# A retention and sliding-window attention trunk: the first retention head of each block goes from seven products with weight sums to eight plain ones

## What is computed

```
layer 0, retention (4 heads, q and k 256 wide, v and gate g 512 wide each):
  h = x @ ret_w_in ;  q, k, v, g = split(h) ;  q, k = rope(q), rope(k) / 16
  per chunk: inner = (q k^T * decay) v ; cross = (q state) * xi
             state = state * g_chunk + (k * zeta)^T v
  r = normalise(inner + cross) ;  x = post_norm(x, (silu(g) * r) @ ret_w_out)
shared keys and values:  kv = x @ swa_w_kv   (4 kv heads, 64 wide)
layer 1, sliding-window attention (16 heads, window of 2 chunks of 64, sinks, relative bias):
  x = post_norm(x, (attention(x) * silu(gate)) @ swa_w_out)
```

## Time and profile before

| | us |
|---|---|
| median of 3 runs | 2418.47 |
| profiled execution | 2420.02 |
| its span, first to last instruction | 2418.1 |
| PE busy | 2322.8 (96%) |
| DVE busy | 1799.0 (74%) |
| ACT busy | 1195.3 (49%) |
| POOL busy | 340.8 (14%) |

### The profile page before, as it was taken

The page is one execution under the profiler, slowest core; times in us unless marked ns, Lnnn a source line. Parts: engine busy times, 40 slices in busy tenths (PEclk is TensorE's granted clock), DMA queues, the critical chain, the costliest instruction groups (busy, mean ns, idle before and its releaser), DMA issues.

```text
span 2418.1 us, 31064 instructions
## 1 busy us (share of the span) xinstructions
PE 2322.8 (96%) x11506; PEld 1889.1 (78%) x11506; DVE 1799.0 (74%) x2589; ACT 1195.3 (49%) x1777; POOL 340.8 (14%) x350
## 2 busy tenths in 40 slices
PE   7888989999999999999999999999999999999996
PEld 5677778877778888887777888888777888888775
DVE  7877878875886668884687666887478667788458
ACT  3433445347644445535754544553665445554463
POOL 4122111203001110111201011110120110011031
PEclk9999999999999999999999999999999999999998
DMA  9886676772664445754284544585248345354423
GB/s 331 280 299 251 228 243 219 251 261 70 235 209 148 131 131 174 255 159 153 92 287 144 170 146 133 169 278 179 75 152 274 116 138 166 124 191 147 122 79 122
DMA packets 215062, 443.38 MB, mean 183 GB/s; under 512 B 15041, under 2 KB 52433, under 8 KB 211329
## 3 DMA queue, kind: packets, MB, share of 16 engines
q1 hardware_dynamic: 200832, 375.58, 47.3%
q0 software_dynamic: 14080, 65.83, 7.4%
HBM read 379.75 MB, written 57.41 MB: 181 GB/s over the span
## 4 chain that ended last, share of the span: by engine, by line
PE 70%; DVE 15%; DMA 6%; issue 4%; ACT 3%; SPq 1%; POOL 0%; DVEq 0%; ACTq 0%; POOLq 0%
PE accs L663 19%; PE accs L664 19%; PE accs L665 19%; DVE w_lo L1301 4%; DMA stage<-t_prep 3%; PE bank L663 2%; PE bank L665 2%; PE bank L664 2%; ACT w_hi L972 2%; PE bank L890 2%; PE bank L899 1%; PE bank L909 1%; PE bank L754 1%; DMA stage<-ret_w_in 1%; PE bank L842 1%
## 5 line engine op out<-in xcount | busy, mean ns | idle before, releaser
L1301 DVE TENSOR_TENSOR w_lo<-stage,w_hi 128x1024 fp32r<-128x1024 f32 x536 | 668.4, 1254 | 367.8 <-ACT w_hi L972 366.7
L972 ACT ACTIVATE w_hi<-stage 128x1024 fp32r<-128x1024 f32 x536 | 561.9, 1058 | 468.4 <-DMA stage<-t_prep 224.4
L663 PE MATMUL accs<-w_hi,xs 128*128 128x512 f32 x1120 | 447.9, 400 | 30.8 <-ACT sg L977 9.5
L665 PE MATMUL accs<-w_hi,xs 128*128 128x512 f32 x1120 | 441.2, 394 | 0.0
L664 PE MATMUL accs<-w_lo,xs 128*128 128x512 f32 x1120 | 440.3, 393 | 0.0
L663 PEld LDWEIGHTS accs<-w_hi,xs 128*128 128x128 f32 x1120 | 213.1, 190 | 81.0 <-issue 28.7
L665 PEld LDWEIGHTS accs<-w_hi,xs 128*128 128x128 f32 x1120 | 212.7, 190 | 45.9
L663 PE MATMUL accs<-x_hi,w_hi 128*128 128x512 f32 (+1 forms) x640 | 245.6, 384 | 1.2 <-ACT sgT L977 0.8
L664 PEld LDWEIGHTS accs<-w_lo,xs 128*128 128x128 f32 x1120 | 213.3, 190 | 42.5
L1961 POOL TENSOR_TENSOR rstd<-ve,half 128x1 f32<-128x1 f32 x96 | 79.4, 828 | 1176.0 <-DVE ve L1357 951.4
L664 PE MATMUL accs<-x_lo,w_hi 128*128 128x512 f32 (+1 forms) x640 | 237.5, 371 | 0.0
(11 more groups left out here) (193 smaller groups left out, 3866.9 us busy)
## 6 DMA issues: line engine op xcount, KB each, us to landing
stage<-t_prep SPq DMA_DIRECT2D x224, 512.0 KB, 4.4
stage<-ret_w_in SPq DMA_DIRECT2D x96, 512.0 KB, 3.9
stage<-ret_w_in SPq DMA_DIRECT2D x128, 256.0 KB, 3.0
stage<-swa_w_in SPq DMA_DIRECT2D x64, 512.0 KB, 4.1
t_prep<-t_buf POOLq DMA_DIRECT2D x28, 1024.0 KB, 6.1
stage<-ret_w_out SPq DMA_DIRECT2D x48, 512.0 KB, 3.7
cs<-rope_t SPq DMA_DIRECT2D x16, 1024.0 KB, 7.5
t_buf<-ret_w_in POOLq DMA_DIRECT2D x32, 512.0 KB, 9.8
```

Of the source, the lines that this page charges most:

```text
L663: mm(dst, lhs[0], rhs[0], start=start, stop=False, skip_group_check=reopened)
L665: return mm(dst, lhs[1], rhs[0], start=False, stop=stop, skip_group_check=reopened)
L972: copy(w_hi[:, g % HS], stage[:, g % LS], ACT.Copy).then_inc(w_hi_made, 1)
L1301: nc.vector.tensor_tensor(w_lo[:, g % LS], stage[:, g % LS], w_hi[:, g % HS].bitcast(F32), sub).then_inc(w_split, 1)
```

## The change

The first head of every block (`plain_head`) computes v and g by eight plain slots of 24 matmuls (4 banks x 2 k tiles x 3) from raw weights and raw x, 192 in place of 168. Slots `VG+8` to `VG+13` of head 0 are vacant: no engine has weight work there, and the ring is counted over the 128 slots that are left (`RING`, `ahead`, `before`), so that head 1's first pairs follow directly.

With it:
- v goes from the banks straight to `v_hi` and `v_lo`, the gate by one Silu from the banks to `sg`; the four sums over partial products and the extra copies of that head are gone. `score(H, 0)` stands at `VG+2`, `retain` at `VG+4`, `VG+5`, `VG+6`.
- Sets 0 to 3 are not made at all. The other 24 are made at other slots; for some the first two of the four operations and the last two stand at different slots ("begin" and "end").
- Block 0's x sums are made by DVE before the first slot, and their splits stand one to two slots earlier. In later blocks two of the four loads of x sums stand at slots 6 and 9 in place of 1 and 3.
- The unused `w_cache` path is removed.

```diff
+PLAIN = range(VG, VG + 8)
+VACANT = range(VG + 8, HEAD)
+PLAIN_BLOCKS = 4
+def vacant(g):
+    return g // NP < PLAIN_BLOCKS and g % NP in VACANT
+REAL = [g for g in range(NS * NP) if not vacant(g)]
+RING = {g: n for n, g in enumerate(REAL)}
+def ahead(g, n=AHEAD):
+    return REAL[RING[g] + n] if g in RING and RING[g] + n < len(REAL) else NS * NP
...
-T_PLAN = [(0, 0, -1, 1), (1, 1, -1, 1), (2, 2, -1, 2), (3, 3, -1, 2), (4, 0, 8, 11), (5, 1, 9, 13), (6, 2, 10, 14),
+T_PLAN = [(4, 0, 0, -1, 4, 4), (5, 1, 0, -1, 5, 5), (6, 2, 0, 1, 6, 6), (7, 3, 0, 2, 7, 7), (8, 0, 0, 6, 9, 10),
+          (9, 1, 0, 7, 11, 11), (10, 2, 0, 8, 18, 18), (11, 3, 0, 9, 19, 19), (12, 0, 0, 12, 19, 19), (13, 1, 0, 13, 20, 20),
+          (14, 2, 0, 20, 29, 31), (15, 1, 0, 22, 31, 34), (16, 3, 0, 21, 36, 36), (17, 2, 0, 33, 37, 37),
+          (18, 3, 0, 38, 47, 49), (19, 2, 0, 39, 49, 52), (20, 3, 0, 51, 54, 54), (21, 2, 0, 54, 56, 56),
+          (22, 3, 0, 56, 65, 65), (23, 3, 0, 67, 72, 72),
...
+def retain_slots(H):
+    return (VG + 4, VG + 5, VG + 6) if plain_head(H) else (VG + 7, VG + 10, VG + 13)
...
+            def plain_vg_pair(s, p):
+                j, i = divmod(p - VG, 4)
+                wait_weights(s * NP + p)
+                for m in range(4):
+                    if i == 0:
+                        fill = VG + (4 * j if m < 2 else 2 + 4 * j)
+                        need(pe, acc_free[m], prior(s, fill, m))
+                    for u in range(2):
+                        k = 2 * i + u
+                        phys = m // 2 if k < 4 else (2, 6)[m // 2]
+                        cols = slice(m % 2 * P, (m % 2 + 1) * P)
+                        mm = mm3(acc[m], (xs[:, phys, 0, k % 4, cols], xs[:, phys, 1, k % 4, cols]), weights(s * NP + p, u),
+                                 k == 0, k == KD - 1)
+                    if m == 1:
+                        mm.then_inc(products, 1)
+                mm.then_inc(products, 1 if p < PLAIN[-1] else 1 + 2 * len(VACANT))
...
+                        if v == 4 and plain_head(H):
...
+                            act.wait_ge(products, used(s * NP + VG + 2) + 1)
+                            copy(v_hi[:, 0:2, :], accs[:, 0:2, :], ACT.Copy).then_inc(v_hi_made, 1)
+                            act.wait_ge(products, used(s * NP + VG + 3))
+                            copy(v_hi[:, 2:4, :], accs[:, 2:4, :], ACT.Copy).then_inc(v_hi_made, 1)
+                            make_hi(ahead(g))
...
+                        if plain_head(H) and v == 4:
+                            nc.vector.tensor_tensor(v_lo[:, 0:2, :], accs[:, 0:2, :], v_hi[:, 0:2, :].bitcast(F32),
+                                                    sub).then_inc(x_free, 2)
+                            dve.wait_ge(v_hi_made, 2 * H + 2)
+                            nc.vector.tensor_tensor(v_lo[:, 2:4, :], accs[:, 2:4, :], v_hi[:, 2:4, :].bitcast(F32),
+                                                    sub).then_inc(y_free, 2)
```

More of the change, by code:

```diff
@@ L122, with before, plain, plain_head @@
 AHEAD, LOAD_AHEAD = 3, 4
[L124 to L135, removed]
+PLAIN = range(VG, VG + 8)
[7 more added lines that the diff above has]
+    return REAL[RING[g] + n] if g in RING and RING[g] + n < len(REAL) else NS * NP
+def before(g, n):
+    return REAL[RING[g] - n] if RING[g] >= n else -1
+def plain(s, p):
+    return s < PLAIN_BLOCKS and p in PLAIN
+def plain_head(H):
+    return H % RH == 0 and H // RH < PLAIN_BLOCKS
+def in_seven(H):
+    return H + 1 - min(H // RH + 1, PLAIN_BLOCKS)
 def loads(g):
-    return 2 if ready_made(g) or PAIRS[g % NP][0] == "qk" else 1
-LOADED, KEEPS, SPLITS = [], [], []
+    return 0 if vacant(g) else 2 if PAIRS[g % NP][0] == "qk" else 1
+LOADED, SPLITS = [], []
 for _g in range(NS * NP):
-    LOADED.append((LOADED[_g - LS] if _g >= LS else 0) + 16 * loads(_g))
-    KEEPS.append((KEEPS[_g - LS] if _g >= LS else 0) + 32 * to_keep(_g))
-    SPLITS.append((SPLITS[-1] if SPLITS else 0) + (not ready_made(_g)))
+    LOADED.append(0 if vacant(_g) else (LOADED[before(_g, LS)] if RING[_g] >= LS else 0) + 16 * loads(_g))
+    SPLITS.append((SPLITS[-1] if SPLITS else 0) + (not vacant(_g)))
 def n_state(n):
@@ L386, in last_set, with weight_pair @@
         def last_set(b):
[L388 to L393, removed]
+            return [n for n, buf, _, load, _, _ in T_PLAN if buf == b and load < RO][-1]
         def set_of(kind, h):
             return {"vg": 4 * h, "ro": RO_SET, "so": SO_SET}[kind]
-        def weight_pair(p, part):
+        def weight_pair(s, p, part):
+            if plain(s, p):
+                j, i = divmod(p - VG, 4)
+                return w_vg[:, i // 2, 2 * (i % 2):2 * (i % 2) + 2, j, 0, :]
             kind, c, q, i = PAIRS[p]
@@ L926, in _ @@
                         continue
-                    if kind in ("vg", "ro", "so"):
+                    if plain(s, p):
+                        plain_vg_pair(s, p)
+                    elif vacant(s * NP + p):
+                        continue
+                    elif kind in ("vg", "ro", "so"):
                         strassen_pair(s, p)
@@ L1756, in _ @@
                             if h == 0:
-                                make_lo(g + AHEAD)
-                        if v == 3:
+                                make_lo(ahead(g))
+                        if not plain_head(H) and v == 3:
                             dve.wait_ge(products, full(s, p, 1))
@@ L1778, in _ @@
                                 .then_inc(y_free, 2)
-                        if v == 11:
+                        if not plain_head(H) and v == 11:
                             after_retain(H, 1)
@@ L1994, in _ @@
                 pool.wait_ge(x_loaded[w], 16)
-            for n in range(4):
-                load_t(n)
+            for n, _, in_block, at_slot, _, _ in T_PLAN:
+                if at_slot < 0:
+                    load_t(n, in_block, at_slot)
             pool.wait_ge(init_done, 3)
```

296 lines of the change are left out of this document (151 added, 145 removed), and 5 rows, old and new, of the table T_PLAN.

## The result

| | before | changed |
|---|---|---|
| median of 19 runs each, us | 2420.28 | 2427.27 |
| lowest and highest, us | 2417.20, 2429.98 | 2423.69, 2430.38 |
| profiled execution: time, span, us | 2420.02, 2418.1 | 2430.38, 2428.3 |

The ratio is 1.0023, 95% interval [1.0016, 1.0031]: 3.9 to 7.5 us slower, though the time lost in block 0 did shrink.

A forecast was written before the change was run, and what follows sets the result against it. The prediction took the number of matmuls on PE (busy 96%) as the bound. Later blocks +13.9 and block 0 -6.1 gave +7.8 us on 2420.0: 2427.8 profiled, 2426 median, range 2410 to 2437.

The forecast's parts named there:

- The extra matmuls: Head 0's vg, every block: 24 more matmuls at 0.227 us, not hidden, 5.45 us a block, 21.8 us in all.
- The third rival: Extra matmuls run at the mean weight load, 0.164 us: 15.8 us instead of 21.8, time 2420, no change; chance 0.04.
- Later blocks: Blocks 1 to 3: extra matmuls 16.4, old waits gone -6.3, new waits 2.1 and 1.7: +13.9 us (bounds 12 to 20).
- The waits for banks 2 and 3: First plain slot, later blocks: PE waits for DVE's second rope product, 0.4 to 1.2 us, 2.1 for three blocks.
- The retention rival: Retention too tight: two tiles a block late by 2 us each in four blocks, +16, 2442 us; chance 0.10.
- Head 0 of block 0: qk -2.0 us; vg 60.8 instead of 71.31, -10.5, with a wait of about 4 us at `VG+4` and 1.9 for clock.
- Head 1, qk: Block 0: `copy_r` waits for set 12's store behind the gate product; qk about 35 instead of 27.94, +7.0 us.
- Head 1, vg: Block 0: +1.9 us at the lower clock, +1.0 for a half set at `VG+7`; other waits left as they are.
- Head 2: Block 0: set 15 stored early, qk -4.2 us; vg -1.7 for clock and -1.4 for a set's wait: -7.3 us.
- Head 3 and ro: Block 0: set 21 one slot later, about +0.8 us; set 23 stored late holds ACT's copy in ro, +3.0 us.
- The sum: Whole kernel: +13.9 in later blocks, -6.1 in block 0, +7.8 us: 2427.8 for the profiled execution, 2426 for the median.
- The first rival: Block 0: VectorE keeps up and no set delays PE, 21 us less, 2405; chance 0.20.

The follow-up runs named there:

- v1_plan: Changed kernel with a new plan of where sets are made, stores ahead of gate products, plain head in all four blocks: ratio 0.9956 to the kernel before.
- v2_one_block: `v1_plan` with the plain head in block 0 alone and sets 0 to 3 made in its head 3: ratio 0.9925 to the kernel before.
- v3_best: `v2_one_block` with set 16 loaded at slot 18 instead of 14 and the bias copy moved from slot 30 to 46: median 2396.75 us, ratio 0.9904.
- e8_bias_late: Changed kernel with only the copy of the bias table moved from slot 30 to slot 46: ratio 1.0030 to the kernel before.

## Why the prediction was right, point by point

- **The extra matmuls**, 0.227 us each with nothing to hide them: 0.227 where it could be read cleanly. The third rival (0.164), which would have given no change, is ruled out in these stretches. This term made the sign. The Trainium skill's 131 ns for such a matmul ("TensorE: Matmul & The Clock Gate", section "Back-to-back issue gap") does not agree with these traces either.
- **Later blocks**: +13.9 forecast, +13.7 measured, and 57.8 to 58.2 us against the 57 to 59 named. The waits for banks 2 and 3 were 0.35 and 0.17 us and none in block 3, a little under 0.4 to 1.2; the wait at `VG+4` was 0.52 us in each block, forecast 0.55. The retention rival (2442) did not occur.
- **Head 0 of block 0**: qk -1.6 for -2.0. The wait for `v_lo` at `VG+4` was 4.11 us where 4 was said, from set 7, as the experiment shows. The clock behind it cost 2.6 us for 1.9; vg came to 62.65 for 60.8.
- **Head 1, qk**: 36.54 us for 35, with rT released by the store behind the gate product, as said. The step missed 2.69 us for the state in the same qk, behind the two more sets.
- **Head 1, vg**: it grew by 0.3 us where 1.9 + 1.0 stood, and this is two misses that cancel. The prediction left the waits as they were; they fell from 9.6 us in all to 5.3. It put 1.9 us on the lower clock; the granted clock of the stretch went from 1.00 to 0.90, and PE's busy time for the same matmuls from 51.18 to 56.09 us. Head 1 together is +8.9 for +9.9, and that it is so close is luck.
- **Head 2**: qk 26.99 for 27, -4.3 for -4.2. vg -1.6 for -3.1: the wait for the gate fell from 2.46 to 1.15 us, which is the -1.4 said, but the -1.7 for the clock did not come. The granted clock is 0.97 in both kernels; the slow time only moved from the start of the stretch to the wait for `v_lo` at its end.
- **Head 3 and ro**: the copy into rT did not wait for set 23. Its store had landed 5.3 us after its issue at 381.10, and ScalarE came to the copy at 386.47, 15.7 us after ro's start. The prediction had the store 20 us after it, and its term of +3.0 did not occur; ro grew by 1.3. Head 3 and kv took 4.8 us more for 0.8 said; some 3 of these are absent in four of the five other kernels with the same code there, and present in the fifth.
- **The sum**: 2427.8 for the profiled execution, which took 2430.38; 2426 for the median, which is 2427.27. Block 0 gained 2.0 in the profile for 6.1 said. By the medians, 7.0 in all less 13.7 in later blocks, it gained 6.7, if these blocks cost the same in every run. The later blocks came as reasoned. In block 0 single terms were off by 1 to 4 us both ways, so that its total fits the median is in part luck.
- **The first rival** (2405) described what the plan can be, not what it was: with the sets in other places and the stores first, the same four plain heads took 2412. The wait for `v_lo` at `VG+4` was still 1.40 us there.

Still open: why the medians of two experiments (24 fewer matmuls, set 12 first) show less than their stretches, and in which blocks the wait for `att_lo` in a seven-product vg of head 0 comes to 2 or 3 us.

## What to carry to other kernels

An exchange of one product for less side work is paid in every block and earned only where the side work is late. Here nearly all such waits were in block 0, and the version with the plain form there and seven products elsewhere was the fastest. No run has the new plan with seven products in block 0 too, so it isn't shown that the plain head earns anything once the sets and the stores stand well: moving the stores alone made the kernel before 0.18% faster. And before exchanging arithmetic, look at where side work stands in the queues: a store behind a product that it doesn't need, or a load that waits in front of work that others need, each made one stretch of PE 4 to 9 us longer. Moving the stores made the whole 4 to 5 us shorter, less than the stretches gained, since other stretches grew.

## What the runs showed of the hardware

- Behind a wait of 4.11 us PE was at its lower level (1.2 GHz): 0.427 us from one 512-column matmul to the next for 5.6 us, against 0.227 before it. With set 7 moved, the waits of 1.32 and 1.88 us in the same stretch left the granted clock at 1.00, and behind 2.40 us at 35.69 the matmuls came at full pace. But in the same trace the wait of 2.41 us at 156.88 was followed by 3.4 us at the lower level, and so was the wait of 2.35 us at 190.22. So the length of one wait does not tell the clock behind it.
- A store of 1 MB from GpSimd's queue landed 7.7 us after its issue with a second one just ahead of it (125.1 to 132.8). The median over the changed kernel's 24 is 6.1 us.
- The copy of the bias table, 0.8 MB in rows of 768 bytes, is followed by a wait of PE of 2.4 to 6.6 us that ends 14 to 21 us after its issue, in head 1 (changed kernel, `v1_plan`, `v2_one_block`) as in head 2 (`v3_best`, `e8_bias_late`). Only `e8_bias_late` moves it alone; in the others loads of sets run beside it.
- In the fastest version's qk of head 1 the DMA engines are busy 0.96 of the time at 361 GB/s and PE waits for nothing; at 0.73 and 251 GB/s, in the changed kernel, it waited 6.5 us (2.69 and 3.83). The share of DMA did not tell whether PE would wait; the order in the queues did.
